# Eight seven-product quads instead of seven in six column pairs of an encoder layer, with the quads in another order

## What is computed

```
h = rms_norm(x, norm_g);  q, k, v, z = split(h @ w_in)      # 4096 x 10240
o = windowed attention of q, k, v (32 heads, 8 kv heads, |t - s| <= 128, ALiBi, sink)
x1 = x + (o * silu(z)) @ w_out                               # 4096 x 4096: the output stage
gate = sigmoid(rms_norm(x1, ple_norm_g) @ w_gate)            # 4096 x 4096: the gate stage
out = x1 + (p @ w_proj) * gate
```

## Time and profile before

| | |
|---|---|
| median of 3 runs | 1661.82 us (1661.6 to 1662.22) |
| the profiled execution | 1661.59 us |
| its span | 1659.6 us, mean granted TensorE clock 0.999 |
| TensorE busy | 1642.9 us, 99% of the span, 7498 matmuls |
| weight loads busy | 1366.7 us, 82% |
| VectorE busy | 1203.0 us, 72% |
| ScalarE busy | 898.7 us, 54% |
| transfers | 328.32 MB, mean 198 GB/s |

### The profile page before, as it was taken

One profiled execution on the slowest core, in us unless ns is written; L12 is line 12 of the kernel. 1 busy time (PEld: TensorE's weight loads), 2 busy tenths in 40 slices (PEclk: granted clock), 3 DMA queues, 4 the chain that ended last, 5 costly groups with the idle time before them and its releaser, 6 DMA issues.

```text
span 1659.6 us, 20741 instructions
## 1 busy us (share of the span) xinstructions
PE 1642.9 (99%) x7498; PEld 1366.7 (82%) x7498; DVE 1203.0 (72%) x1369; ACT 898.7 (54%) x1147; POOL 29.0 (2%) x27
## 2 busy tenths in 40 slices
PE   7999999999999999999999999999999999999998
PEld 6888888888888888888888888888888888888886
DVE  7754556565656656575665779888889978989897
ACT  8443345454454545545454665656566756566564
POOL 1000000000000000000000000000000000000000
PEclk9999999999999999999999999999999999999999
DMA  8666665656556565655656567767666575767674
GB/s 297 199 187 195 196 182 159 196 164 178 166 176 178 163 192 161 184 169 176 179 162 192 162 200 240 243 206 244 209 232 215 199 245 186 259 198 241 215 228 140
DMA packets 137741, 328.32 MB, mean 198 GB/s; under 512 B 10576, under 2 KB 14928, under 8 KB 137680
## 3 DMA queue, kind: packets, MB, share of 16 engines
q1 hardware_dynamic: 136688, 327.20, 63.5%
q10 hardware_dynamic: 992, 0.31, 0.1%
HBM read 319.08 MB, written 8.39 MB: 197 GB/s over the span
## 4 chain that ended last, share of the span: by engine, by line
PE 99%; DVE 1%; DMA 0%; ACT 0%; issue 0%; SPq 0%; DVEq 0%
PE bank L1421 18%; PE bank L1423 18%; PE bank L1422 18%; PE bank L1579 13%; PE bank L1581 13%; PE bank L1582 13%; PE bank L1492 1%; PE bank L1444 1%; PE bank L1436 1%; PE bank L1482 0%; PE bank L1481 0%; PE bank L1480 0%; PE bank L1648 0%; PE bank L1501 0%; PE bank L1502 0%; PE bank L1649 0%
## 5 line engine op out<-in xcount | busy, mean ns | idle before, releaser
L885 DVE TENSOR_TENSOR w_lo<-raw,w_hi 128x1024 fp32r<-128x1024 f32 x320 | 391.3, 1223 | 315.3 <-ACT w_hi L506 314.1
L506 ACT ACTIVATE w_hi<-raw 128x1024 fp32r<-128x1024 f32 x320 | 339.1, 1060 | 390.6 <-PE bank L1423 387.6
L1421 PE MATMUL bank<-w_lo,aT_hi 128*128 128x512 f32 x1280 | 502.9, 393 | 8.7 <-DVE w_lo L885 8.7
L1423 PE MATMUL bank<-w_hi,aT_lo 128*128 128x512 f32 x1280 | 499.6, 390 | 0.0
L1422 PE MATMUL bank<-w_hi,aT_hi 128*128 128x512 f32 x1280 | 499.4, 390 | 0.0
L1421 PEld LDWEIGHTS bank<-w_lo,aT_hi 128*128 128x128 f32 x1280 | 241.0, 188 | 57.0 <-issue 8.7
L1423 PEld LDWEIGHTS bank<-w_hi,aT_lo 128*128 128x128 f32 x1280 | 240.9, 188 | 50.6
L1422 PEld LDWEIGHTS bank<-w_hi,aT_hi 128*128 128x128 f32 x1280 | 241.2, 188 | 48.4
L1579 PE MATMUL bank<-w_lo,aT_hi 128*128 128x512 f32 x676 | 263.8, 390 | 0.0
L1582 PE MATMUL bank<-w_hi,aT_lo 128*128 128x512 f32 x676 | 263.2, 389 | 0.0
L1581 PE MATMUL bank<-w_hi,aT_hi 128*128 128x512 f32 x676 | 263.2, 389 | 0.0
(11 more groups left out here) (211 smaller groups left out, 1673.7 us busy)
## 6 DMA issues: line engine op xcount, KB each, us to landing
raw<-in_w_in_dram SPq DMA_DIRECT2D x320, 512.0 KB, 3.6
raw<-in_w_out_dram SPq DMA_DIRECT2D x100, 512.0 KB, 4.4
raw<-in_w_gate_dram SPq DMA_DIRECT2D x90, 512.0 KB, 5.1
stage<-in_w_gate_dram SPq DMA_DIRECT2D x38, 512.0 KB, 5.1
stage<-in_w_out_dram SPq DMA_DIRECT2D x28, 512.0 KB, 5.4
out_dram<-arena SPq DMA_DIRECT2D x7, 1024.0 KB, 5.4
stage<-in_xT_dram SPq DMA_DIRECT2D x8, 512.0 KB, 8.4
arena<-in_x_dram SPq DMA_DIRECT2D x4, 1024.0 KB, 7.5
```

The lines of the kernel that those rows point to most:

```text
L506: nc.scalar.activation(w_hi[:, i % RING, :], raw[:, i % RING, :], ACT.Copy).then_inc(hi_done, 1)
L885: nc.vector.tensor_tensor(w_lo[:, i % RING, :], raw[:, i % RING, :], w_hi[:, i % RING, :].bitcast(F32), ALU.subtract).then_inc(lo_done, 1)
L1421: nc.tensor.matmul(outs[t][:, :], ahi, wlo, start=first and jj == 0, stop=False)
L1423: last = nc.tensor.matmul(outs[t][:, :], alo, whi, start=False, stop=final and jj == 1)
```

## The change

Pairs 1 to 3 of both stages now have all eight odd quads in the seven-product form. Their order is 0, 2, 4, 1, 6, 3, 8, 5, 7, 10, 9, 12, 11, 13, 14, 15; in the last pair of the gate stage 15 stands ahead of 14. So two, in that last pair three, seven-product quads now follow each other directly in places, and `ahead` holds for those too: the sums are then made behind the last unit of the quad ahead. The third set of combinations in pair 0 takes chunks 0 to 3, not 1 to 3, as does S1. The arena's buffers lie at other addresses, and both halves of a pair's w_proj block pass through one raw buffer, so the load of half 1 stands one pair later in SP's queue. The conversions of output pair 3 stand at positions 5 to 12, and the last gate pair has its steps where the other two have theirs.

```diff
-N_EXT = QUADS // 2 - 1
-X_CHUNKS, Z_CHUNKS, Y_CHUNKS = (4, 6), (6, 8), (1, 4)
+N_EXT = QUADS // 2
+X_CHUNKS, Z_CHUNKS, Y_CHUNKS = (4, 6), (6, 8), (0, 4)
 def strassen_from(stage, m):
-    return 9 if m == 0 else 3
+    return 9 if m == 0 else 1
 def order_of(stage, m):
-    if (stage, m) != (GATE, PAIRS - 1):
+    if m == 0:
         return list(range(QUADS))
-    order = [0, 1]
-    for i in range(3, QUADS, 2):
-        order += [i, i - 1]
-    return order
+    last = [15, 14] if (stage, m) == (GATE, PAIRS - 1) else [14, 15]
+    return [0, 2, 4, 1, 6, 3, 8, 5, 7, 10, 9, 12, 11, 13] + last
...
-        wp_raw = [stage4[:, 2:4, 1, :], at(9472, 1024).rearrange("q (a n) -> q a n", a=PLE_T)]
+        wp_raw = [stage4[:, 2:4, 1, :]] * 2
...
                     if m < PAIRS - 1:
                         sp.wait_ge(wp_split, 2 * m + 2)
-                        for b in range(2):
-                            load_wp(m + 1, b, wp_raw[b])
+                        load_wp(m + 1, 0, wp_raw[0])
+                elif n == 1 and s == GATE and m > 0:
+                    sp.wait_ge(wp_split, 2 * m + 1)
+                    load_wp(m, 1, wp_raw[1])
...
-                        ahead = qs[pos + 1] if not q.strassen and pos + 1 < QUADS and qs[pos + 1].strassen else None
+                        ahead = qs[pos + 1] if pos + 1 < QUADS and qs[pos + 1].strassen else None
                         for h in range(q.units):
                             lo_unit(q, h)
-                            if ahead and h == 0:
+                            if ahead and h == q.units - 2 + q.strassen:
                                 weight_sums_1(ahead)
-                            elif ahead:
+                            if ahead and h == q.units - 1:
                                 weight_sums_2(ahead)
...
-                                elif m == PAIRS - 1 and 3 <= pos < 11 and h == q.units - 1:
-                                    conv_lo_pair(GATE, pos - 3)
+                                elif m == PAIRS - 1 and 5 <= pos < 13 and h == q.units - 1:
+                                    conv_lo_pair(GATE, pos - 5)
...
-                                elif (pos, h) == ((1, 1) if m == PAIRS - 1 else (2, 0)):
+                                elif (pos, h) == (2, 0):
                                     wp_lo_part(m, 1)
                                     gate_products(m - 1)
-                                elif (m, pos, h) in ((1, 4, 0), (2, 4, 0), (3, 3, 1)):
+                                elif (pos, h) == (4, 0):
                                     outputs(m - 1, 0)
-                                elif (m, pos, h) in ((1, 8, 1), (2, 8, 1), (3, 9, 1)):
+                                elif (pos, h) == (8, 1):
                                     outputs(m - 1, 1)
```

More of the change, by code:

```diff
@@ L94 @@
     sums_free: int = 0
+    first: bool = False
     @property
@@ L139, in plan @@
         if q.strassen:
-            q.slots = (2, 3, 4, 5) if (q.stage, q.pair, q.pos) in ((GATE, 0, 9), (GATE, PAIRS - 1, 2)) else (4, 5, 2, 3)
+            q.slots = (2, 3, 4, 5) if (q.stage, q.pair, q.pos) == (GATE, 0, 9) else (4, 5, 2, 3)
             q.nth = nth
+            q.first = not any(p.strassen for p in table[q.stage][q.pair][:q.pos])
             nth += 1
@@ L604, in ext_hi_part @@
                 act.wait_ge(comb, 3 * s + count)
-                nc.scalar.activation(ext_hi[:, lo - 1:hi - 1, :, :].rearrange("q e k t -> q (e k t)"), combos_of[chunks],
+                nc.scalar.activation(ext_hi[:, lo:hi, :, :].rearrange("q e k t -> q (e k t)"), combos_of[chunks],
                                      ACT.Copy).then_inc(ext_top, 1)
@@ L610, in conv_hi_pair @@
                 if s == GATE:
-                    q = pair_quads(OUT, PAIRS - 1)[i]
+                    q = next(q for q in pair_quads(OUT, PAIRS - 1) if q.i == i)
                     act.wait_ge(pe_half, ends(q, q.units - 1))
@@ L863, in _ @@
                                     wp_hi_part(m, 1)
[L864 to L870, removed]
+                                elif (pos, h) in ((2, 1), (3, 1)):
+                                    pj_copy(m, pos - 2)
                             if s == GATE and m < PAIRS - 1 and (pos, h) == (14, 1):
@@ L1116, in weight_sums_1 @@
                 dve.wait_ge(lo_done, q.sums_free)
-                if q.pair == 0 and q.i == strassen_from(q.stage, 0):
+                if q.pair == 0 and q.first:
                     dve.wait_ge(ext_done, 3 * q.stage + 3)
-                elif q.stage == GATE and q.i == strassen_from(GATE, q.pair):
+                elif q.stage == GATE and q.first:
                     dve.wait_ge(evac, evac_base(GATE, q.pair - 1) + GATE_OPS)
@@ L1155, in ext_lo_part @@
                 dve.wait_ge(ext_top, 3 * s + count)
-                nc.vector.tensor_tensor(ext_lo[:, lo - 1:hi - 1, :, :].rearrange("q e k t -> q (e k t)"), combos_of[chunks],
-                                        ext_hi[:, lo - 1:hi - 1, :, :].rearrange("q e k t -> q (e k t)").bitcast(F32),
+                nc.vector.tensor_tensor(ext_lo[:, lo:hi, :, :].rearrange("q e k t -> q (e k t)"), combos_of[chunks],
+                                        ext_hi[:, lo:hi, :, :].rearrange("q e k t -> q (e k t)").bitcast(F32),
                                         ALU.subtract).then_inc(ext_done, 1)
@@ L1548, in ext_tile @@
             def ext_tile(i, k):
-                e = (i - 3) // 2
+                e = i // 2
                 return ext_hi[:, e, k, :], ext_lo[:, e, k, :]
@@ L1613, in strassen_unit @@
                         pe.wait_ge(conv_lo, QUADS * q.stage + i + 1)
-                    if q.pos == strassen_from(q.stage, q.pair):
+                    if q.first:
                         pe.wait_ge(ext_done, 3 * q.stage + 3)
-                    if q.pair == 1 and i == 3:
+                    if q.first and q.pair == 1:
                         pe.wait_ge(s1_done, q.stage + 1)
```

14 lines of the change are left out of this document (7 added, 7 removed).

## The result

The changed kernel takes **1664.25 us** (median of 22 runs, 1663.23 to 1665.35) against 1662.11 us of the kernel before in the same comparison (22 runs, 1661.25 to 1662.72). The ratio is 1.0014, with a 95% interval of 1.0008 to 1.0019: slower by some 2 us, and inside 0.2%. The forecast was 1664.9, in a range of 1661.9 to 1667.8. What was forecast as a difference was +3.1 us, and +2.14 was measured; the kernel before took 1662.11 us in this comparison and 1661.82 in the runs that the forecast started from, which brings the two totals 0.3 closer than the differences are. The profiled execution took 1665.35 us, the longest of the 22; its span is 1663.5 us, the granted clock 0.999.

What follows compares the result with a forecast made beforehand. TensorE, 99% busy, bounds the kernel through its matmul count and any waits for VectorE. Terms: -4.08 + 0.70 + 0.17 + 0.17 + 1.89 + 0.32 + 1.14 + 1.79 + 1.02 = +3.1 us, so 1664.9, range 1661.9 to 1667.8.

Steps and rivals of the forecast that it cites:

- The 18 matmuls: TensorE, six changed pairs: a dense quad (D) becomes seven-product (S), three matmuls fewer each; -4.08 us without added waits.
- The cap of 0.60 us: Second of two S in a row shares four slots; VectorE's lead over TensorE's weight load capped at 0.60 (0.3 to 0.8).
- rival A: All VectorE work is hidden, only the 18 matmuls count: 1657.7 us; needs a slot round trip 1.9 us shorter; chance 0.07.
- Output pair 3 and the last pair: TensorE waits for VectorE at quad 13 of output pair 3, +1.89 us, and quad 15 of last gate pair, +1.79.
- a lead of -1.93: Lead change from one S's unit 3 to the next S's unit 0: VectorE takes 3.29 us against TensorE's 1.36.
- The transitions: Starts of the pairs after output pairs 1, 2 and 3: VectorE reaches D1.1 (quad 1, unit 1) later; +0.17, +0.17, +0.32 us.
- S7.2 in the gate pairs: Quad 7's unit 2, gate pairs 1 to 3: two output additions behind S7.1 make its lead -0.38; +1.14 us for three.
- Output pair 0, +0.70: Larger third set of combinations delays quad 7 and the load for quad 8's unit 1; +0.70 us, between 0 and 1.2.
- the end, +1.02: Last gate pair: D14.1's lead of 1.12 frees VectorE at 1647.34, delaying its last chain from 1646.32; +1.02 us.
- Rival C, late loads: Gate weights land after 6.3 us, TensorE waits; 1667.9 at 7.3; sign: ScalarE waiting on raw weights at D10, D12; chance 0.18.

Runs made afterwards that it cites:

- Experiment 1: Changed kernel with one edit: from pair 1 on, units take the six slots in turn; 1659.49 us, ratio 0.9985 to the kernel before.
- kernel 8: Changed kernel with slots in turn, conversions one quad earlier in output pair 3, quad 1's combinations apart in output pair 0, and the early x1 reload; 1658.62 us.
- experiment 2: Changed kernel with the two additions of outputs(m - 1, 1) moved earlier, behind unit 1 of dense quad 6; 1663.28 us, ratio 1.001.
- experiments 3: Kernel before, own order and seven quads, with the larger third set (4 chunks), new addresses and one raw w_proj buffer; 1662.42 us, ratio 1.0003.
- 6: Changed kernel with quad 1's combinations made apart and later in output pair 0, the third set again chunks 1 to 3; 1663.34 us, ratio 1.0009.
- kernel 5: Changed kernel with the last pair's reload of x1's second half sent to a raw buffer free behind quad 13; 1663.75 us, ratio 1.0012.
- 4: Changed kernel with output pair 3 in the old order, seven seven-product quads and conversions at positions 3 to 10; 1662.16 us, ratio 1.0003.
- 7: Changed kernel with slots in turn, plus output pair 3's eight conversions one quad earlier, at positions 4 to 11; 1659.1 us, ratio 0.9985.
- 9: Kernel 8 with output pair 3's last two conversions behind positions 13 and 14, not 10 and 11; 1658.35 us, ratio 0.9978.

## Why the prediction held, and where it did not

**The 18 matmuls, -4.08 us.** Right: output pair 1, where nothing waits, is 0.68 us shorter, three matmuls of 0.227.

**The cap of 0.60 us.** Right, and it decides: in the rows of gate pair 1 above it is 1437.84 less 1437.24. Experiment 1 shows it by taking it away. It is also the condition that the prediction named for rival A (1657.7): with a longer way round before a slot is used again the time falls to 1659.49, and kernel 8 comes within 1 us of A.

**Output pair 3 and the last pair, +1.89 and +1.79.** Right in mechanism and place, a little small. The two pairs are 0.13 and 0.08 us longer than forecast. The step from an S to an S directly behind it was taken as a lead of -1.93; here it is -2.05 (S11.3's subtraction ends at 1278.72, S13.0's 4.01 later, of which 0.60 are a conversion: 1.36 - 3.41). Almost all of the difference lies at the first sum, which has to wait because the scratch buffer that it writes is read by the subtraction ahead. The prediction counted 0.11 us for that wait, as between two sums; here it costs 0.21. VectorE's rows of output pair 3, from S11.2 to S13.0's subtraction:

```profile
1276.36 2.36 DVE L1107 TENSOR_TENSOR w_lo<-arena,w_hi 128x1024 fp32r<-128x1024 f32 x2
1278.85 1.23 DVE L1119 TENSOR_TENSOR arena<-raw 128x1024 f32<-128x1024 f32 x1
1280.11 0.69 DVE L1126 TENSOR_TENSOR arena<-raw,arena 128x512 f32<-128x512 f32 x1
1280.84 0.69 DVE L1128 TENSOR_TENSOR arena<-raw,arena 128x512 f32<-128x512 f32 x1
1281.45 0.68 DVE L1077 TENSOR_TENSOR aT_lo<-stage,aT_hi 128x512 fp32r<-128x512 f32 x1
1282.05 0.68 DVE L1107 TENSOR_TENSOR qT_lo<-raw,qT_hi 128x512 fp32r<-128x512 f32 x1
```

The first sum begins at 1278.85, 0.13 after the subtraction's end at 1278.72, the second only 0.03 after the first one's end (1280.08, 1280.11), and an operation that waits for nothing begins 0.08 ahead of the end of the one before it (1281.45 against 1281.53). Ahead of the first sum, and of neither of the others, VectorE's queue runs a wait of its own (EVENT_SEMAPHORE, L1113, 0.05 us from 1278.76). The last pair has the same: S13.3's subtraction ends at 1640.34, the sum begins at 1640.47, S15.0's ends at 1643.75, and 1.36 less those 3.41 is -2.05. The Trainium skill says that a semaphore between operations costs nothing extra ("VectorE: DVE Perf Modes", "The DRAIN you can't avoid"). By that the step would be -1.60; both places contradict it with -2.05.

**The transitions, +0.17, +0.17, +0.32.** Right: -0.53 in output pair 2 (forecast -0.51), +0.29 in gate pair 0. Output pair 1's share appears in pair 2, output pair 2's in pair 3, at D2.1 (1220.98).

**S7.2 in the gate pairs, +1.14.** Right, 0.39 in pairs 1 and 2 and 0.37 in the last, shown by experiment 2.

**Output pair 0, +0.70.** Right, +0.73, shown by experiments 3 and 6.

**The step that failed: the end, +1.02.** I gave D14.1 a lead of 1.12, the value of a D followed by an S. But D14 is the last quad, no sums stand behind its units, and its lead is 2.23: VectorE is done with it at 1649.43 (1647.08 + 2.35), and its first weight load comes at 1651.66 (1654.15 less 11 matmuls). With 2.23 in the prediction's own sum VectorE is free at 1648.54 - 2.23 = 1646.31, and its last chain began at 1646.32: just in time. So it doesn't delay the chain, and in kernel 5, where no transfer is late, the stretch is 8.56 us. What the changed kernel lost there in its profile, 0.73, was the wait for the reload of x1, which the prediction does not name at all. The size came near by luck, and in the profile alone. In the medians nothing of it is seen: the changed kernel is 2.14 us over its kernel before, the pairs alone account for 2.30, and kernel 5, without the late reload, is 2.08 over its own. Without this term the sum would have been 2.1 us and the forecast 1663.9.

**Rival C, late loads.** Half of its sign is there: ScalarE waits 1.46 and 1.90 us on the raw weights of D12.1 in gate pairs 1 and 2. But VectorE turns to that unit only 1.39 us after ScalarE has it done (1451.65 against 1450.26), and no wait of TensorE comes of it. In the last gate pair ScalarE waits 0.58 and 1.35 us on raw weights, again without one. Gate weights landed in 5.4 us in the median (5.1 before).

## What to carry to other kernels

Where buffers are reused by a fixed plan, work out for every unit how long the way round is: slot free, high part, low part, first use. If two units in a row share buffers, that time caps the lead whatever came ahead, and mean load says nothing of it. Saving work on the bound engine by giving more to its helper pays only where the lead can bear it; a stall sits at the first place where the lead runs out, and work moved ahead of that place changes nothing, work moved behind it only carries the stall on to the next. And compare stage by stage: here most pairs agree to hundredths of a microsecond, whereas the untouched first part alone scatters by more than a microsecond.

## What the hardware did that I had not expected

After a stall TensorE makes good a little of it: the second weight load follows the first 0.11 us behind (1282.79, 1282.90) and only the third at the usual 0.23 (1283.13). The load of 1283.92 (the next at 1284.03) does the same. So a stall costs what it shows less 0.04, which lies between any two loads, less 0.12. At D8.1 of output pair 0 that makes 0.72 of 0.88, and the pair is 0.73 us longer than before.

How long a transfer takes to land varies from execution to execution. The reload of 512 KB is issued at 1647.19 in the changed kernel and lands 5.6 us later; VectorE's addition then begins at 1652.94. In kernels 1, 2, 4, 6 and 7, issued behind the same subtraction, it lands after 5.1, 4.9, 4.3, 4.8 and 5.0 us. Where it is issued 5 to 10 us earlier against the end, it took 3.9 us (kernels 5 and 9), 3.7 (3 and 8) and 3.8 (the kernel before). Why was not looked into.
